# Gate norms applied behind the product, a reordered router, rotary loads inside the first mixture of experts, and a gated convolution product amid the taps

## The reference

```python
def rms_norm(x, g):
    return x * lax.rsqrt(jnp.mean(x * x, axis=-1, keepdims=True) + EPS) * g

for i in range(2):
    xn = rms_norm(h, g_mix[i])
    h = h + (conv_module if i == 0 else nsa_attention)(xn, ...)
    h = h + hier_moe(rms_norm(h, g_ffn[i]), ...)      # router: xn @ w_rg + b_rg, xn @ w_re + b_re
    gate = sigmoid(rms_norm(h, g_ple[i]) @ ple_w_gate[i])
    h = h + gate * (p[i] @ ple_w_proj[i])
```

## Time and profile before

| | us |
|---|---|
| median of 3 runs | 1322.99 |
| lowest and highest | 1318.56, 1326.4 |
| the profiled execution, whole | 1329.65 |
| its span, first to last instruction | 1327.7 |

### The profile page before, as it was taken

The page is one execution under the profiler, slowest core; times in us unless marked ns, Lnnn a source line. Parts: engine busy times, 40 slices in busy tenths (PEclk is TensorE's granted clock), DMA queues, the critical chain, the costliest instruction groups (busy, mean ns, idle before and its releaser), DMA issues.

```text
span 1327.7 us, 27879 instructions
## 1 busy us (share of the span) xinstructions
PE 1037.3 (78%) x10412; PEld 591.1 (45%) x10413; DVE 321.4 (24%) x890; ACT 302.5 (23%) x710; POOL 455.8 (34%) x743
## 2 busy tenths in 40 slices
PE   6968977767777776778998789786776778678678
PEld 6744544333344433334455554443343444344443
DVE  3994300000021000005136671310010131000011
ACT  5873311111111111112112571211111111112121
POOL 2340164343355434330000130344344464353520
PEclk9989988888898888888999699988888899888989
DMA  9942499999999999998324605699999999999980
GB/s 303 384 192 56 183 398 429 428 429 428 428 428 418 427 428 430 428 416 309 131 64 185 259 4 210 275 390 430 428 428 427 429 428 421 430 427 422 429 341 32
DMA packets 63160, 449.24 MB, mean 338 GB/s; under 512 B 10873, under 2 KB 21745, under 8 KB 38288
## 3 DMA queue, kind: packets, MB, share of 16 engines
q1 hardware_dynamic: 58064, 448.25, 81.7%
q10 hardware_dynamic: 5056, 0.48, 0.3%
HBM read 447.66 MB, written 1.05 MB: 338 GB/s over the span
## 4 chain that ended last, share of the span: by engine, by line
DMA 43%; PE 39%; DVE 9%; issue 4%; ACT 3%; SPq 1%; POOL 0%; ACTq 0%; DVEq 0%
DMA ring<-in_moe_w_up 43%; PE PS L569 15%; PE PS L454 10%; PE PS L548 2%; PE PS L584 2%; ACT arena L1140 1%; PE PS L556 1%; PE PS L591 1%; DVE hn L1408 1%; PE PS L442 1%; PE PS L738 1%; DVE arena L1408 1%; DVE ppw L1754 1%; SPq L321 1%; PE PS L515 1%
## 5 line engine op out<-in xcount | busy, mean ns | idle before, releaser
L569 PE MATMUL PS<-ring,arena 128*32 128x256 f32 x4160 | 332.7, 484 | 184.1 <-DMA ring<-in_moe_w_up 153.6
L569 PEld LDWEIGHTS PS<-ring,arena 128*32 128x32 f32 x4160 | 160.9, 134 | 348.0 <-issue 217.1
L1460 DVE TENSOR_TENSOR arena<-PS,arena 64x256 f32<-64x256 f32 x65 | 27.8, 428 | 578.2 <-ACT arena L1204 571.3
L584 PE MATMUL PS<-ring,arena 128*32 128x256 f32 x2080 | 125.7, 381 | 30.8 <-DVE arena L1463 30.8
L1204 ACT ACTIVATE arena<-PS 64x256 f32<-64x256 f32 x64 | 24.2, 378 | 506.5 <-PE PS L569 506.5
L975 POOL TENSOR_SCALAR arena<-arena 128x32 f32<-128x32 f32 x64 | 18.9, 295 | 282.9 <-PE PS L556 278.5
L934 POOL TENSOR_SCALAR arena<-arena 128x512 f32<-128x512 f32 x67 | 105.7, 1578 | 24.5 <-POOL arena L981 12.9
L584 PEld LDWEIGHTS PS<-ring,arena 128*32 128x32 f32 x2080 | 73.1, 109 | 61.1 <-issue 37.4
L928 POOL TENSOR_SCALAR arena<-arena 128x32 f32<-128x32 f32 x260 | 88.7, 364 | 13.1 <-POOL arena L975 12.9
L936 POOL TENSOR_TENSOR arena<-arena 128x512 f32<-128x512 f32 x67 | 85.7, 1279 | 5.6
L591 PE MATMUL PS<-arena 32*128 32x256 f32 x1040 | 74.5, 397 | 6.6 <-ACT arena L1202 0.6
(11 more groups left out here) (325 smaller groups left out, 1216.4 us busy)
## 6 DMA issues: line engine op xcount, KB each, us to landing
ring<-in_moe_w_up SPq DMA_DIRECT2D x62, 2048.0 KB, 22.3
ring<-in_moe_w_down SPq DMA_DIRECT2D x62, 2048.0 KB, 24.0
ring<-in_moe_w_gate SPq DMA_DIRECT2D x60, 2048.0 KB, 17.9
wb<-in_ple_w_gate SPq DMA_DIRECT2D x4, 2048.0 KB, 33.1
ring<-in_conv_w_pw SPq DMA_DIRECT2D x3, 2048.0 KB, 18.8
ring<-in_nsa_w_in SPq DMA_DIRECT2D x3, 2048.0 KB, 16.2
wb<-in_moe_w_gate SPq DMA_DIRECT2D x2, 2048.0 KB, 14.5
wb<-in_moe_w_up SPq DMA_DIRECT2D x2, 2048.0 KB, 11.0
```

Of the source, the lines that this page charges most:

```text
L569: i = pe.matmul(PS[32 * j:32 * j + 32, BGU, 0:256].rearrange("q (p c) -> q p c", c=2), xT[:, k, :], w[:, k, :].rearrange("q (p h c) -> q h ...
L584: i = pe.matmul(PS[32 * j:32 * j + 32, BY, 0:Q4], hT[:, c, 32 * f:32 * f + 32], w_dn(s)[:, f, c, Q4 * j:Q4 * (j + 1)], start=(q == 0), sto ...
L1460: return v.tensor_tensor(hh[64:128, :], PS[64:128, BGU, 0:256], gs[64:128, :], ALU.mult)
```

## The change

Five edits.

1. In the PLE of both layers PE transposes `h` itself, each quarter as soon as it is copied out of the accumulators; the scaling of `hn` goes, and 1/rms becomes the per-token scale of the sigmoid.
2. In the router tile 1 is transposed from `h` as well. DVE multiplies its 36 logits by 1/rms and adds the bias (now on all partitions). The scaled `hn` of tile 1 is still made, later, since `gather` reads it.
3. PE's order around the router is new (below), and so is ACT's: it copies the gathered rows and the weight rows ahead of the accumulator copies, but behind the last quarter of the embedding product.
4. The five small loads for the rotary tables are issued in the first expert loop, behind the loads of expert 19; `before` is read only for experts with extra rounds.
5. The gated products of convolution chunks 4 to 7 are issued by DVE after the eighth tap of the chunk before.

The rest of the diff merges counters of the attention and changes no order there.

```diff
+GLU_AHEAD = 4
-        rowb = sb("rowb", [1, DEPTH * (NG + NE)])
+        rowb = sb("rowb", [P, DEPTH * (NG + NE)])
                 pair(m + 1, (2, 0))
+                if L == 0:
+                    sp.wait_ge(pp_ok, 4)
+                    for i, v in enumerate((nsa_q_norm[0:1, :], nsa_k_norm[0, 1:2, :], nsa_k_norm[0, 2:3, :], nsa_k_norm[0, 0:1, :])):
+                        sp.dma_start(gn[:, i, :], v.broadcast_to([P, DH])).then_inc(rot_in, 16)
+                    sp.dma_start(invb, inv_freq.broadcast_to([P, DH // 2])).then_inc(rot_in, 16)
...
             def norm_T(a, t):
-                pe.wait_ge(hn_act if t else hn_dve, a + 1)
+                after_moe, late_tile = a in (2, 5), a in (1, 4) and t == 1
+                if not (after_moe or late_tile):
+                    pe.wait_ge(hn_act if t else hn_dve, HN_AT[a])
                 for k in range(KD):
+                    if after_moe and k % 2 == 0:
+                        pe.wait_ge(h_act if k % 4 else h_dve, (H_ACT if k % 4 else H_DVE)[a] - 1 + k // 4)
+                    if late_tile and k % 4 == 0:
+                        pe.wait_ge(h_dve, H_DVE[a] - 1 + k // 4)
                     i = pe.transpose(PS[:, 4 + 2 * t + k // 4, (k % 4) * P:(k % 4 + 1) * P],
-                                     hn[:, t, k * P:(k + 1) * P], ident[:, :])
+                                     (h if after_moe or late_tile else hn)[:, t, k * P:(k + 1) * P], ident[:, :])
...
+                pe.wait_ge(h_dve, H_DVE[a] - 2)
+                embedding_product(L, 0, 0, 0)
+                norm_T(a, 1)
                 pe.wait_ge(misc_in, 16 * N_MISC)
+                router_product(L, 0)
+                router_product(L, 1)
+                embedding_product(L, 0, 0, 1)
+                for n, t in ((0, 1), (1, 0)):
+                    for c in range(2):
+                        embedding_product(L, n, t, c)
+                embedding_product(L, 1, 1, 0)
...
-                pe.wait_ge(rt_s, 2 * L + 1)
-                rows(W4, 7).then_inc(rt_row, 1)
+                pe.wait_ge(xt_act, 2 * a + 2)
+                pe.wait_ge(rt_s, 2 * L + 2)
+                rows(S4, 6).then_inc(rt_row, 1)
+                pe.wait_ge(hn_act, HN_AT[a])
                 pe.wait_ge(sel_ok, (NE + 2) * L + 1)
-                gather(sel[0]).then_inc(ga_mm, 1)
+                gather(sel[0], between=extra_rounds).then_inc(ga_mm, 1)
+                embedding_product(L, 1, 1, 1)
                 pe.wait_ge(xg_ok, g0 + 1)
                 xg_T().then_inc(xt_mm, 1)
+                rows(W4, 7).then_inc(rt_row, 1)
...
-                norm_half(a)
+                square_sum(a)
                 xnT_copy(a, ROW_FFN + 8 * L, 1)
+                scale_half(a)
...
                 products(1)
+                act.wait_ge(ga_mm, g0 + 1)
+                nc.scalar.copy(xg, PS[:, BGX, 0:Q4]).then_inc(xg_ok, 1)
+                act.wait_ge(rt_row, 3 * L + 3)
+                nc.scalar.copy(wrow, PS[:, 7, :].rearrange("p (a q) -> p a q", a=2)).then_inc(row_act, 1)
                 act.wait_ge(pp_ok, 4 * (L + 1))
                 for j in range(4):
                     nc.scalar.copy(PS[:, ACC + j, :].rearrange("p (t q) -> p t q", t=2),
                                    h[:, :, Q4 * j:Q4 * (j + 1)]).then_inc(acc_ok, 1)
...
+                        act.wait_ge(rs_ok, RS_BEFORE[a + 1] + t + 1)
+                        nc.scalar.activation(hn[:, t, 512 * n:512 * (n + 1)], PS[:, 2 * n + t, :], ACT.Sigmoid,
+                                             scale=rstd[:, 1, t:t + 1]).then_inc(pl_sig, 1)
...
+                    if w == DVE_TAPS // 2 and GLU_AHEAD <= c + 1 < KD:
+                        glu(c + 1)
...
+                dve.wait_ge(rs_ok, RS_BEFORE[a] + 2)
+                link(v.scalar_tensor_tensor(out=R[:, 1, 0:36], in0=R[:, 1, 0:36], scalar=rstd[:, 1, 1:2], in1=rowb[:, 36 * L:36 * (L + 1)],
+                                            op0=ALU.mult, op1=ALU.add))
```

More of the change, by code:

```diff
@@ L64 @@
 H_ACT = [0, 0, 2, 2, 2, 4, 4]
[L66 removed]
+HN_AT = [1, 2, None, 3, 4, None]
 RS_BEFORE = [0, 2, 4, 6, 9, 11]
@@ L463, in embeddings_T, with embedding_product, router_product @@
                 i.then_inc(ptr, 1)
-            def embedding_product(L, n, t):
-                if (n, t) == (0, 0):
-                    pe.wait_ge(pT_ok, L + 1)
-                    pe.wait_ge(h_dve, H_DVE[3 * L + 1])
-                for c in range(2):
-                    i = pe.matmul(PS[:, 2 * n + t, :], pT2[:, c, t * P:(t + 1) * P],
-                                  wproj[:, c, 512 * n:512 * (n + 1)], start=(c == 0), stop=(c == 1))
-                i.then_inc(pp_mm, 1)
+            def embedding_product(L, n, t, c):
+                i = pe.matmul(PS[:, 2 * n + t, :], pT2[:, c, t * P:(t + 1) * P],
+                              wproj[:, c, 512 * n:512 * (n + 1)], start=(c == 0), stop=(c == 1))
+                if c == 1:
+                    i.then_inc(pp_mm, 1)
+            def router_product(L, t):
+                a = 3 * L + 1
+                o = PS[:, BGU, 64 * t:64 * t + 36]
+                if t == 0:
+                    xnT_ready(a, 0, 0)
+                    pe.matmul(o, ones[0:1, :], rowb[0:1, 36 * L:36 * (L + 1)], start=True, stop=False)
+                for k in range(KD):
+                    xnT_ready(a, k, t)
+                    i = pe.matmul(o, xnT[:, k, t * P:(t + 1) * P], wr[:, L, k, :], start=(t == 1 and k == 0), stop=(k == KD - 1))
+                if t == 1:
+                    i.then_inc(rt_mm, 1)
             pe.wait_ge(const_ok, 1)
@@ L550, in _, with gather @@
                     i.then_inc(out_mm, 1)
-            def gather(lhs):
+            def gather(lhs, between=None):
                 for t in range(NT):
+                    if t == 1 and between is not None:
+                        between()
                     rows = hn[:, t, :].rearrange("q (p j c) -> q j p c", j=4, c=2)
@@ L596, in moe @@
                 a = 3 * L + 1
+                pe.wait_ge(pT_ok, L + 1)
+                pe.wait_ge(h_dve, H_DVE[a] - 2)
+                embedding_product(L, 0, 0, 0)
+                norm_T(a, 1)
                 pe.wait_ge(misc_in, 16 * N_MISC)
-                xnT_ready(a, 4, 0)
-                xnT_ready(a, 0, 0)
-                for t in range(NT):
-                    if t == 1:
-                        embedding_product(L, 0, 0)
-                        embedding_product(L, 0, 1)
-                        norm_T(a, 1)
-                    o = PS[:, BGU, 64 * t:64 * t + 36]
-                    pe.matmul(o, ones[0:1, :], rowb[0:1, 36 * L:36 * (L + 1)], start=True, stop=False)
-                    for k in range(KD):
-                        xnT_ready(a, k, t)
-                        i = pe.matmul(o, xnT[:, k, t * P:(t + 1) * P], wr[:, L, k, :], start=False, stop=(k == KD - 1))
-                i.then_inc(rt_mm, 1)
-                embedding_product(L, 1, 0)
-                embedding_product(L, 1, 1)
-                pe.wait_ge(xt_dve, 2 * a + 2)
-                pe.wait_ge(xt_act, 2 * a + 2)
+                router_product(L, 0)
[5 more added lines that the diff above has]
+                embedding_product(L, 1, 1, 0)
                 pe.wait_ge(const_ok, 2)
@@ L1212, in moe @@
                                    PS[:, ACC + j, :].rearrange("p (t q) -> p t q", t=2)).then_inc(h_act, 1)
-                norm(a + 1, ROW_PLE + 8 * L)
+                xnT_copy(a + 1, ROW_PLE + 8 * L, 0)
+                square_sum(a + 1)
+                xnT_copy(a + 1, ROW_PLE + 8 * L, 1)
                 if L == 0:
@@ L1226, in _ @@
             moe(0)
-            norm_half(3)
+            square_sum(3)
+            scale_half(3)
             for t in range(NT):
@@ L1262, in kT_copy @@
                                PS[:, 6 + b % 2, :].rearrange("p (k q) -> p k q", k=2)).then_inc(qt_act, 1)
-            act.wait_ge(c1_x, 1)
-            nc.scalar.activation(sq[:, 512:768], sq[:, 256:512], ACT.Sigmoid, scale=2.0 * float(np.sqrt(2.0 / np.pi))).then_inc(c1_s, 1)
+            act.wait_ge(c1_d, 1)
+            nc.scalar.activation(sq[:, 512:768], sq[:, 256:512], ACT.Sigmoid, scale=2.0 * float(np.sqrt(2.0 / np.pi))).then_inc(c1_a, 1)
             kT_copy(0, 1)
@@ L1585, in moe @@
                                   PS[:, ACC + j, :].rearrange("p (t q) -> p t q", t=2)).then_inc(h_dve, 1)
-                norm(a + 1, ROW_PLE + 8 * L)
+                xnT_copy(a + 1, ROW_PLE + 8 * L, 0)
+                square_sum(a + 1)
+                dve.wait_ge(ssq_ok, a + 2)
+                mean_square(1)
+                xnT_copy(a + 1, ROW_PLE + 8 * L, 1)
                 if L == 0:
```

99 lines of the change are left out of this document (46 added, 53 removed).

## The result

The change gained about half of what was forecast. That is 7.5 to 9 us where 16.3 were forecast. The median misses the predicted 1306.7 by 11.2 us. 7.1 of these are the sum's. The rest is the base's: the forecast took 6.7 us off the profiled execution to get the median, and here the two lie 2.5 apart (over 26 runs the median before was 1324.93, not 1322.99). The profiled execution took 1320.43 us, span 1318.5 (before 1329.65 and 1327.7), so between the two profiles there are 9.2 us to explain.

The account below looks back on a forecast made before the run. Bound: full transfer engines in the expert loops; PE, or PE and DVE by turns, between them. Terms -12.8 - 1.5 - 1.6 + 0.6 - 1.0 = -16.3 us gave a median of 1306.7, 8-in-10 range 1300 to 1315.

Parts of the forecast that it names:

- Convolution: Gated products ahead of their chunk: earlier end against a wait in chunk 3, -1.0 us, bounds -3.4 and +0.4.
- DVE's end: Convolution: a 4.2 us sigmoid wait less shorter sums puts DVE's end 2.6 us later, at 101.0.
- The 3.4 us that the forecast saw at the convolution's end: DVE's 2.65 us wait for ACT's copies and PE's taps, with the sums behind: 3.4 us to be had.
- Router: Mixer's end to first expert: earlier logits less PE's longer new order, -1.5 us in layer 1, -1.6 in layer 2.
- The slots `S4` ... come 3.4 earlier: First router: the slots, before at 154.7 us, come at 151.3.
- Rival B: Weight rows and late accumulator copies swallow the routers' gains: profiled execution 1309.8 us; chance 0.14.
- PLEs: Both layers' PLEs: gate product starts earlier and PE's clock stays up, -6.6 and -6.2 us, together -12.8.
- the two signs that were to prove the forecast wrong: Last scatter to end not 6 us shorter than the 42 before, or the expert loops starting no earlier.
- Rival A: Clock stays at 1.2 GHz through the start of both PLE gate products: sum -10.7 us, 1312.3; chance 0.22.
- D: PLEs: first sigmoids wait for POOL's power, gate products end no earlier; about 1320 us; chance 0.03.
- C: First experts: added code-fetch stalls of 5.2 us each; five make +9.7, 1332.7 us; chance 0.05.
- Rotary loads: Five small loads moved into the full first expert loop cost +0.6 us, bounds 0.3 and 1.2; nothing comes back.

Follow-up runs that it names:

- `b_router`: Kernel before with only the change's router part; PLEs, convolution and rotary loads as before: 1325.28 us, ratio 0.9993 to the kernel before.
- `b_ple`: Kernel before with only the change's PLE part (transposes from the residual, scale in the sigmoid): 1315.39 us, ratio 0.9913 to the kernel before.
- `a_nople`: Changed kernel with the PLEs put back as before; router, convolution and loads as changed: 1329.71 us, ratio 1.0044 to the kernel before.
- `a_gap`: Changed kernel with PE's first transposes in each PLE held until the norm's power is done: 1326.26 us, ratio 1.0007 to the kernel before.

## Why the prediction was wrong

The sign and the largest term were right; the size and the time were not. The step that failed most is the convolution's, 3.9 of the 7.1 us missed.

**Convolution (-1.0 forecast, +2.9 measured, outside the bounds of -3.4 to +0.4).** The step read "DVE's end: +4.2 - 0.3 - 1.3 = +2.6, to 101.0". The wait and the shorter sums were right: 4.28 us, and the seven sums fell from 6.3 to 4.3 us. What was missing is where the overlap went. POOL's building of the tap matrices did not end when the sums moved clear of it; it now fell on the taps:

```profile
L1432 DVE SCALAR_TENSOR_TENSOR hn<-ppw,arena,hn 128x256 f32<-128x256 f32 x45 | 26.5, 588 | 0.0
L1432 DVE SCALAR_TENSOR_TENSOR arena<-ppw,arena 128x256 f32<-128x256 f32 x43 | 25.6, 596 | 0.0
```

Before (busy us and mean ns stand behind the first bar):

```profile
L1408 DVE SCALAR_TENSOR_TENSOR hn<-ppw,arena,hn 128x256 f32<-128x256 f32 x44 | 24.3, 553 | 0.0
L1408 DVE SCALAR_TENSOR_TENSOR arena<-ppw,arena 128x256 f32<-128x256 f32 x43 | 23.5, 546 | 0.0
```

That is +4.3 in the taps, 0.5 of it one record that the trace before lacks, so +3.8, against -2.0 in the sums. With +4.0 for the wait it makes +5.8; DVE's end moved by 5.6. Taps of more than 0.5 us number 6 or 7 in every kernel with none or one product ahead and 13 or 14 in every kernel with four. The second error follows: "chunk 7's gated product comes earlier" held only if DVE lost less than half a chunk on the way, and it lost more. The groups of kernels put the order's own cost at 2.3 us; what is left of the 2.9 is mostly a later start, which no step of the forecast could have held. The 3.4 us that the forecast saw at the convolution's end were there for the most part: one product ahead gets 2.8 of them. The edit put 5.6 us of wait and slower taps on DVE, the engine that bounds the convolution, to give time to ACT and PE, which wait for it.

The Trainium skill (SBUF — State Buffer, Terms) says that DVE and GpSimd have one port pair between them, held for a whole instruction, and that the loser waits. The rows agree in kind: a tap that comes every 0.40 us alone took 0.87, 1.19 or 2.50 where POOL ran beside it. An overlap moved is not an overlap removed.

**Router (-1.5 and -1.6 forecast; with the loops +1.2 and -0.2 measured, against -0.9 and -1.6).** The step read "The slots `S4` ... come 3.4 earlier". It let DVE set the start of the counting. In front of it stand six embedding matmuls; one is two records, 0.87 us, not 0.44, so they take 5.2 us at the full clock, level with DVE's 5.3. In layer 2 the slots came 2.9 earlier against the mixer's end. In layer 1 the low clock fell on them (7.81 us) and S4 came 0.3 later. A cover with no width to spare was counted as one. From S4 to the first expert it took 6.6 and 7.7 us for the forecast 7.4. Rival B, "the routers' gains are swallowed", describes this, though the weight rows and late copies were not what did it. `b_router` shows that nothing is left in the time.

**PLEs (-12.8 forecast, -11.8 measured).** The mechanism was right: start of the product, clock, 16 records and power ahead of the sigmoid came as named. The product starts 0.2 us later than forecast and takes 7.1, not 6.87; twice both is 0.9 of the 1.0 missing. Of the two signs that were to prove the forecast wrong, the first is met by a little: the end is 5.7 us shorter, not 6. The second is met for the first loop, which starts 3.4 us later than before (164.42 for 160.98), not for the second, which starts 4.3 earlier. `b_ple`, `a_nople` and `a_gap` show it from three sides. Rival A (clock low all the same) and D are out; C (more fetch stalls) is out: the same stalls are there, 5.88 us in layer 1 (before 5.23), 2.48 and 3.62 in layer 2 (before 0.96 and 4.42).

**Rotary loads (+0.6 forecast, +1.0 by the groups of kernels).** "After the loop nobody waited for them, so nothing comes back" was wrong: with the PLE shortened DVE would have waited, and 1.4 us comes back. The chain before could not show it, for there the slower norm covered the loads.

**Attention (0 forecast, -1.2 measured).** Before, the clock stood at 0.50 in the window of 726 to 728 us and after it stood at 1.00 in the matching one; `b_ple`, with the low clock there too, shows no gain in this stretch. The same stretch, with no edit in it, took 190.4 to 195.6 us in the thirteen kernels, so the 1.2 us are within what it varies by from kernel to kernel, and no gain of the change is shown. That the clock's place makes the spread is likely and not shown.

Open: what sets the low clock's place in a stretch in which PE does not stand, and 2 to 4 us of `a_nople`'s loss.

## What to carry to other kernels

Ask of an edit on a staged loop what the switch from one order to the other costs, once, on the engine that bounds the stage, and move only the iterations for which the inputs are already there: one product ahead at the end gained 2.8 us where four ahead lost 2.3. Compare kernels at a mark behind the stretch that the clock can slow, or a low clock that only changed its place is read as a cost. When an instruction moves clear of a shared resource, say what moves into its place. When work is put in the cover of another engine, compare both lengths record by record; equal lengths are no cover, and a fall of the clock turns them into a loss.

## What the runs showed of the hardware that was not expected

- The granted clock fell to 0.50 while PE, as the profile counts it, was busy in 10.00 of 10.00 us (145 to 155 us of the kernel after), at the same place in a second run of it. The Trainium skill (TensorE: Matmul & The Clock Gate, Part 1) ties the low clock to an idle PE; `a_gap` agrees (a fall behind 0.38 us of work in 4), the router does not.
- Ahead of the second expert PE stood without a releaser for 2.61 to 5.98 us in thirteen kernels whose expert code differs hardly.
- From the first refill of the ring to the loop's end every kernel took 433.0 to 436.4 us in either loop, whatever lay ahead of it.
